# A two-layer decoder trunk on one core: the last two output tiles of each residual stage as token-half jobs, the norm behind them and the next quad by token halves

## What is computed

```python
hn = rmsnorm(x, norm1_g) * (1.0 + sc1) + sh1
proj = hn @ w_in                       # 1024 -> 2560, split in xl, gl, bs, cs, hs
...                                    # convolutions, gates, a recurrence -> lru_out, sc_out
mix = jnp.concatenate([lru_out, sc_out], axis=-1) @ w_out
x = x + g1 * mix
hn2 = rmsnorm(x, norm2_g) * (1.0 + sc2) + sh2
u, v = jnp.split(hn2 @ ffn_w_up, 2, axis=-1)       # 1024 -> 2 x 2816
uc, new_fc = causal_conv(u, st_fc, ffn_conv_w)
x = x + g2 * ((jax.nn.gelu(uc) * v) @ ffn_w_down)
```

## Time and profile before

| | |
|---|---|
| time, median of 3 runs (lowest, highest) | 1374.34 us (1372.85, 1374.78) |
| the profiled execution: its own time | 1370.7 us |
| its span, first to last instruction | 1369.0 us |
| mean granted TensorE clock | 0.981 of 2.4 GHz |
| TensorE matmuls, busy | 1324.8 us, 97% |
| weight loads, busy | 1262.4 us, 92% |
| VectorE, busy | 701.0 us, 51% |
| ScalarE, busy | 467.1 us, 34% |

### The profile page before, as it was taken

One profiled execution on the slowest core, in us unless ns is written; L12 is line 12 of the kernel. 1 busy time (PEld: TensorE's weight loads), 2 busy tenths in 40 slices (PEclk: granted clock), 3 DMA queues, 4 the chain that ended last, 5 costly groups with the idle time before them and its releaser, 6 DMA issues.

```text
span 1369.0 us, 23539 instructions
## 1 busy us (share of the span) xinstructions
PE 1324.8 (97%) x9727; PEld 1262.4 (92%) x9727; DVE 701.0 (51%) x1212; ACT 467.1 (34%) x589; POOL 47.3 (3%) x94
## 2 busy tenths in 40 slices
PE   5799999999999999999989999998999999999998
PEld 3698888889999999999989888998999999999997
DVE  2753663475534544345577158447553354534556
ACT  4523652353321322222353257326331232222332
POOL 3000000000000000000020000000000000000001
PEclk8899999989999999999999999999999999999999
DMA  9444555512122122222232645321222212222212
GB/s 334 165 158 171 203 206 185 185 62 93 61 93 92 62 92 92 69 86 77 76 123 86 211 166 204 124 93 62 73 81 93 93 61 92 81 73 93 75 49 94
DMA packets 108663, 157.02 MB, mean 115 GB/s; under 512 B 3543, under 2 KB 100792, under 8 KB 102453
## 3 DMA queue, kind: packets, MB, share of 16 engines
q1 hardware_dynamic: 101269, 112.56, 24.6%
q0 software_dynamic: 7168, 43.47, 9.2%
q10 hardware_dynamic: 160, 0.05, 0.0%
HBM read 153.08 MB, written 2.99 MB: 114 GB/s over the span
## 4 chain that ended last, share of the span: by engine, by line
PE 94%; DVE 3%; DMA 2%; ACT 1%; issue 0%; DVEq 0%; SPq 0%; POOLq 0%; ACTq 0%
PE ps L335 29%; PE ps L337 28%; PE ps L336 28%; PE ps L394 3%; PE ps L481 1%; DMA ada_w<-in_w_ada 1%; PE ps L428 1%; PE ps L417 1%; DMA work<-in_w_ada 0%; PE ps L358 0%; DVE work L804 0%; PE ps L360 0%; PE ps L359 0%; DVE w_raw L1156 0%; PE ps L409 0%
## 5 line engine op out<-in xcount | busy, mean ns | idle before, releaser
L335 PE MATMUL ps<-norm_hi,w_hi 128*128 128x288 f32 x2048 | 612.5, 299 | 13.7 <-DVE norm_lo L777 13.3
L336 PE MATMUL ps<-norm_lo,w_hi 128*128 128x288 f32 x2048 | 606.6, 296 | 0.0
L337 PE MATMUL ps<-norm_hi,w_lo 128*128 128x288 f32 x2048 | 604.4, 295 | 0.0
L335 PEld LDWEIGHTS ps<-norm_hi,w_hi 128*128 128x128 f32 x2048 | 386.4, 189 | 33.6 <-issue 19.1
L337 PEld LDWEIGHTS ps<-norm_hi,w_lo 128*128 128x128 f32 x2048 | 388.1, 189 | 0.0
L336 PEld LDWEIGHTS ps<-norm_lo,w_hi 128*128 128x128 f32 x2048 | 387.0, 189 | 0.0
L335 PE MATMUL ps<-mid_hi,w_hi 128*128 128x288 f32 x904 | 268.7, 297 | 0.0
L336 PE MATMUL ps<-mid_lo,w_hi 128*128 128x288 f32 x904 | 266.7, 295 | 0.0
L337 PE MATMUL ps<-mid_hi,w_lo 128*128 128x288 f32 x904 | 265.8, 294 | 0.0
L767 DVE TENSOR_TENSOR w_lo<-w_raw,w_hi 128x2048 fp32r<-128x2048 f32 x92 | 210.6, 2290 | 95.0 <-ACT w_hi L539 94.8
L539 ACT ACTIVATE w_hi<-w_raw 128x2048 fp32r<-128x2048 f32 x92 | 175.6, 1909 | 163.7 <-PE ps L337 162.9
(11 more groups left out here) (189 smaller groups left out, 846.7 us busy)
## 6 DMA issues: line engine op xcount, KB each, us to landing
w_raw<-in_ffn_w_up SPq DMA_DIRECT2D x44, 1024.0 KB, 5.1
ada_w<-in_w_ada POOLq DMA_DIRECT2D x40, 1024.0 KB, 5.2
w_raw<-in_w_in SPq DMA_DIRECT2D x20, 1024.0 KB, 5.3
w_raw<-in_ffn_w_down SPq DMA_DIRECT2D x16, 1024.0 KB, 5.2
w_raw<-in_w_out SPq DMA_DIRECT2D x8, 1024.0 KB, 5.2
w_raw<-in_ffn_w_down SPq DMA_DIRECT2D x8, 768.0 KB, 4.6
work<-in_w_ada SPq DMA_DIRECT2D x4, 1024.0 KB, 10.8
work<-in_x_prompt SPq DMA_DIRECT2D x4, 512.0 KB, 5.1
```

The costliest lines, as they stand in the source:

```text
L335: T.matmul(out, WH[:, r, k, c:c + P], xh[:, k, h, :], start=start, stop=False)
L336: T.matmul(out, WH[:, r, k, c:c + P], xl[:, k, h, :], start=False, stop=False)
L337: last = T.matmul(out, WL[:, r, k, c:c + P], xh[:, k, h, :], start=False, stop=stop)
```

## The change

The residual stages keep six output tiles (`FM`) as they are. The last two (`NQ`) run as four jobs of 24 matmuls: first half of tile 6, first half of tile 7, then the second halves. The statistics of the first half stand inside the third job, its spread inside the fourth; those of the second half stand in the next quad. The norm runs first over the first half, for two chunks at a time (`k_pair`), then over the second. `first_quad` does the first half for tiles 0 and 1, then for tiles 2 and 3, and then the same for the second half. The statistics and spreads have banks 4 and 5. The copy of the spread to SBUF is gone. FFN groups are 6, 8, 8 in place of 8, 8, 6, so that the last has eight chunks. At the end, three of the six tiles of `y` are transposed and scaled before the second half's statistics, and `y` is stored in that order.

```diff
-    GROUPS = [8, 8, KF - 16]
+    GROUPS = [KF - 16, 8, 8]
...
+            def half_chunk(i, s, k, h, xh, xl):
+
+                r, c, out = i // 2, (i % 2) * P, PS[:, 2 * s + h, 0:HALF]
+                T.matmul(out, WH[:, r, k, c:c + P], xh[:, k, h, :], start=(k == 0), stop=False)
+                T.matmul(out, WH[:, r, k, c:c + P], xl[:, k, h, :], start=False, stop=False)
+                return T.matmul(out, WL[:, r, k, c:c + P], xh[:, k, h, :], start=False, stop=(k == KX - 1))
+
+            def half_tiles_of_last_two(pair, m, after):
+
+                pe.wait_ge(lo_done, pair + 3)
                 for h in range(2):
...
+                    for i in range(NQ):
+                        pe.wait_ge(psum_free[i], pair + 1)
+                        for k in range(KX):
+                            last = half_chunk(2 + i, i, k, h, MH, ML)
+                            if k == KX - 1:
+                                last.then_inc(tile_done if h else half_done, 1)
+                            after(h, i, k)
+
+            def first_quad(pair, m, after, last_bank):
+
+                for h in range(2):
+                    for tiles in ((0, 1), (2, 3)):
+                        for k in range(KX):
+                            if tiles[0] == 0 and k % 2 == 0:
+                                pe.wait_ge(norm_ready, m * 8 - 8 + h * 4 + k // 2 + 1)
...
+                            for i in tiles:
...
+                                last = half_chunk(i, i, k, h, NH, NL)
+                                if k == KX - 1 and h == 1:
+                                    last.then_inc(tile_done, 1)
+                            after(h, tiles[0], k)
...
+                def norm_in_jobs(m, free):
+
+                    def after(h, i, k):
+                        if (h, i, k) == (1, 0, KX - 3):
+                            pe.wait_ge(*free)
+                            norm_stats(m, 0)
+                        if (h, i, k) == (1, 1, 2):
+                            norm_spread(m, 0)
+                    return after
+
+                def norm_in_quad(m):
+
+                    def after(h, i, k):
+                        if (h, i, k) == (0, 2, 2):
+                            norm_stats(m, 1)
+                        if (h, i, k) == (0, 2, KX - 2):
+                            norm_spread(m, 1)
+                    return after
...
+                for i in range(4):
+                    tile(l * PL + 2 + T_UP[0] // 2, i, NH, NL, range(KX), reads=0 if i < 2 else 1)
...
+            def after_last(h, i, k):
+                if (h, i, k) == (1, 0, KX - 3):
+                    pe.wait_ge(ns_read, L * 6)
+                    norm_stats(L * 2 + 1, 0)
+                if (h, i, k) == (1, 0, KX - 1):
+                    y_tile(0)
+                if (h, i, k) == (1, 1, KX // 2 - 1):
+                    pe.wait_ge(std_ready, 4 * L + 1)
+                    y_tile(1)
+                if (h, i, k) == (1, 1, KX - 1):
+                    pe.wait_ge(y_rows, 1)
+                    y_tile(2)
...
+            pe.wait_ge(y_rows, 3)
+            norm_stats(L * 2 + 1, 1)
...
+                dve.wait_ge(rs_done, max(m * 2 - 1 + h, 2))
                 scaled(0)
...
+                for p in range(5):
+                    if p < 4:
+                        f, t = sm(halves(HID[p % 2])), sm(halves(T1[p % 2]))
+                        step(V.tensor_tensor(f, t, seqs(GS, p, h), ALU.mult))
+                        V.tensor_tensor(f, f, seqs(MOD[:, sh:sh + KX], p, h), ALU.add).then_inc(norm_f, 1)
+                    if p:
+                        dve.wait_ge(norm_hi, n + p)
+                        low(k_pair(NL, p - 1, h), halves(HID[(p - 1) % 2]), k_pair(NH, p - 1, h), norm_ready)
+                    if p < 3:
+                        scaled(p + 1)
+                    fill(p)
...
+            def end_of_first_half(l, e, t, c):
+
+                for i in range(FM, KX):
+                    half_residual(l, e, t, c, i)
+                    sum_square(e, i - 1)
+                sum_square(e, 7)
+                rstd(e + 2, 0)
+                half_residual(l, e, t, c, 8)
+
+            def end_and_norm(l, e, t, c, split1, sh):
+
+                m = e + 2
+                end_of_first_half(l, e, t, c)
+
+                def fill(p):
+                    if p == 0:
+                        half_residual(l, e, t, c, 9)
+                    if p == 1:
+                        sum_square(e, 8)
+                        sum_square(e, 9)
+                    if p in (2, 3):
+                        split_half(m, *split1, p - 2)
+                normalise(m, sh, 0, fill)
+                rstd(m, 1)
+                normalise(m, sh, 1, lambda p: None)
```

More of the change, by code:

```diff
@@ L338, in chunk, with tile @@
                 return last
-            def tile(pair, i, xh, xl, order, ready=None):
+            def tile(pair, i, xh, xl, order, ready=None, reads=1):
                 if i % 2 == 0:
                     pe.wait_ge(lo_done, pair + (i // 2 + 3))
-                pe.wait_ge(psum_free[i % 2], pair + (i // 2 + 1))
+                pe.wait_ge(psum_free[i % 2], pair + (i // 2 + reads))
                 for j, k in enumerate(order):
@@ L349, in tile @@
                 last.then_inc(tile_done, 1)
-            def last_tile(pair, order):
-                pe.wait_ge(psum_free[1], pair + 2)
-                for h in range(2):
-                    out = PS[:, 2 + h, 0:HALF]
-                    for j, k in enumerate(order):
-                        hi, lo = WH[:, 1, k, P:2 * P], WL[:, 1, k, P:2 * P]
-                        T.matmul(out, hi, MH[:, k, h, :], start=(j == 0), stop=False)
-                        T.matmul(out, hi, ML[:, k, h, :], start=False, stop=False)
-                        last = T.matmul(out, lo, MH[:, k, h, :], start=False, stop=(j == len(order) - 1))
-                    last.then_inc(tile_done if h else half_done, 1)
@@ new lines, in _ @@
+                    if g == 2:
+                        for i in range(2):
+                            tile(l * PL + 2 + T_DN[g] // 2, i, MH, ML, range(K))
+                    made += K
+                between = norm_in_jobs(l * 2 + 3, (ns_read, l * 6 + 6))
+                if l < L - 1:
+                    half_tiles_of_last_two(l * PL + T_DN[2] // 2 + FM // 2, l * 2 + 3, between)
+                    first_quad((l + 1) * PL, l * 2 + 3, norm_in_quad(l * 2 + 3), None)
+            def after_last(h, i, k):
[10 more added lines that the diff above has]
+                    y_tile(2)
@@ new lines, in end_and_norm @@
+            def end_and_norm(l, e, split1, sh, between):
+                m = e + 2
+                square(e, 6)
+                square(e, 7)
+                std(m, 0)
+                square(e, 8)
+                norm_round(m, sh, 0, 0)
+                square(e, 9)
+                norm_round(m, sh, 0, 1)
+                split_halves(*split1, part=0)
+                norm_round(m, sh, 0, 2)
+                split_halves(*split1, part=1)
+                norm_round(m, sh, 0, 3)
+                between()
+                std(m, 1)
+                for p in range(4):
+                    norm_round(m, sh, 1, p)
@@ L596, in _ @@
                 A(halves(SQ0[k % 2]), X[:, k], ACT.Square).then_inc(sq_ready, 1)
-            std(1)
+            for h in range(2):
+                std(1, h)
             for l in range(L):
@@ L609, in _ @@
             ada_rows(1, first=True)
+            for part in range(2):
+                split_halves(0, 1, part)
+            for h in range(2):
+                for p in range(4):
+                    norm_round(1, MOD_SH1, h, p)
             for l in range(L):
-                split_halves(l, 1)
-                norm_round(l * 2 + 1, l * 16, MOD_SH1)
+                split(l, 2)
                 for c in range(KH):
@@ L728, in _ @@
                         act.preload_act_table(ACT.Sqrt)
-                        for m in range(KX):
-                            square(l * 18 + 9, m)
+                        for m in range(FM):
+                            square(l * 2 + 1, m)
                             if m in (1, 3):
@@ L1056, in _ @@
                 split(l, 11)
-                for m in range(KX - 1):
+                for m in range(FM):
                     residual(done(l, T_WOUT + m), m % 2, X[:, m], lambda a_, b_, m=m: MOD[:, MOD_G1 + m, a_:b_],
```

401 lines of the change are left out of this document (204 added, 197 removed).

## The result

| | before | after |
|---|---|---|
| time, median (lowest, highest) | 1373.89 us (1372.85, 1374.78), 4 runs | 1385.6 us (1382.56, 1388.17), 4 runs |
| the profiled execution: time, span | 1370.7, 1369.0 us | 1382.56, 1380.9 us |
| TensorE matmuls, busy | 1324.8 us, 97% | 1330.5 us, 96% |

The ratio is 1.0085 with a 95% interval of 1.0066 to 1.0104: slower by 11.7 us. The forecast was 6.65 us, to 1381.0 with a range of 1374 to 1387: the direction was right, the time lies in the range, and the size was not right.

A forecast was written before the change was run, and what follows sets the result against it. TensorE, busy for 97% of the span, bounds the kernel, so its idle time and inserted work count. Terms sum to +6.0 us, with the clock +6.65, giving 1377.3 profiled and 1381.0 us as median; range 1374 to 1387.

The forecast's parts named there:

- Waits at the boundaries: Boundaries 1, 2, 3 follow layer 0's output projection, its FFN, layer 1's output projection: TensorE waits 6.2, 8.1, 8.1 us.
- the 15 that the forecast set as its test: Over the whole kernel, TensorE's waits for low parts summing below 15 us would show the prediction wrong.
- Light work: Statistics and spreads inserted among TensorE's matmuls at each boundary: 0.8 and 1.1 us each, 3.8 a boundary.
- rival (a): Statistics, spreads and transposes slip among dense matmuls at no cost: 14.5 us fall away, 1366.5 us; chance 0.12.
- Rival (b): Low parts not late at boundaries 2 and 3, waits of 0.7 and 2.1 vanish: 1375.4 us; chance 0.13.
- the term of 0.65: Fall of TensorE's clock at the three boundaries: 1.3 us a fall, half of one fall taken, 0.65 us.
- rival (c): Clock falls at all three boundaries and VectorE is late once in each quad by 0.5: 1386.3 us; chance 0.20.
- costs nothing while that holds: FFN group order 6, 8, 8 issues the same matmuls, splits and loads; free while weight loads have no wait.
- The tail: End of the kernel from tile six: 27.6 us against 26.3 for the old order with eight chunks, +1.3.
- +6.0: Sum without the clock: 0.1 at the start, 0.1, 2.3, 2.2 at boundaries 1 to 3, 1.3 in the tail.
- at the start: Start of the kernel: only the third pair late by 0.35 us against a removed 0.27, +0.1.

The follow-up runs named there:

- repeated run: The changed kernel run once more, unaltered, against the kernel before: 1385.88 us, ratio 1.0077.

## Why the prediction was right in direction and short in size

**Waits at the boundaries: right.** Forecast 0.7 (with a restart 0.8), 2.1, 1.0, 1.3, 2.55 and 0.3 at boundaries 2 and 3; measured 1.03, 2.20, 1.04, 1.31 and 2.66 at boundary 2 of the repeated run, where the clock was full in the first half, and nothing for the last. The first low part behind the last job's residual is VectorE's row at 709.05. At boundary 1 the forecast 0.9 became 1.09. The sum of waits for low parts, 16.1 us and 3.2 under another name, is above the 15 that the forecast set as its test.

**Light work: oversized.** 0.8 and 1.1 were charged, 0.68 and 0.97 measured between dense matmuls, so 3.3 a boundary and not 3.8. The term is real, and rival (a), that it is free, is refuted: it needed about a third of the charge, and 87% was measured. Rival (b), low parts in time at boundaries 2 and 3, is refuted by the 2.04.

**The clock: the term of 0.65 was mis-sized most.** The forecast gave each boundary a little over one chance in three at 1.3. The profiled execution shows a fall in all three second halves at 1.0 each (14.43 for 13.42), and one in the tail, 2.2, which had no term at all: 5.2 together. Even by its own chances the forecast was too low: three times a third of 1.3 is 1.3, and it took half of that. This is the clock part of rival (c). The rule of the Trainium skill that I set beside the sum (TensorE: Matmul & The Clock Gate, Why this matters for your kernels) would have left the clock up through these waits, all shorter than the old ones; 18 of 21 second halves below full clock behind 2.66 us decide against it here, while the three at 1.00 show that it does not fail each time. The mistake was mine as well: I took the falls as a share of one event, and did not see that behind the wait stands a dense half, where a slow clock costs time.

**The group order and the loads: "costs nothing while that holds" was the step that failed.** The weight loads indeed had no wait. But I looked only at them, and not at the loads of modulation weights that GpSimd issues. Nor was it the group order (1.0005): the quad by halves gave ScalarE and VectorE its first finished tile later, the split of pair 3 ended 5.2 us later, and a 1 MB load started ahead of the other. The stretches of the two mixing stages are longer by 2.2 + 0.4 = 2.6 us. Rival (c) had VectorE late for the splits; it looked for the wait in the quad, where none came, and so came near the measured time (1386.3) by luck, with the clock's half of its mechanism right and the other not.

**The tail: +1.3 forecast, +0.7 at full clock, +2.9 with the fall.** After the last matmul the forecast's 11.7 was 11.8 in the repeat; the statistics and transposes ahead of it cost (1366.78 - 1351.74) less 95 matmuls of 0.133, so 2.4, and not 3.1.

**The sum, corrected.** The forecast's +6.0 was too high by 0.45 at boundary 1, 0.2 each at boundaries 2 and 3 (light work 0.5 less, waits 0.3 more), 0.3 at the start and 0.6 in the tail: +4.25 is left. To it come the clock, 3.0 + 2.2 = 5.2, and the loads, 2.6, less 0.2 in the FFNs' bodies: 11.85, measured 11.9. Of the 5.2 by which 11.85 exceeds 6.65, the clock makes 5.2 - 0.65 = 4.55 and the loads 2.6; what was priced too high, with the 0.2, takes back 1.95. That the forecast lies as near as it does owes something to this: errors of 7.15 one way and 1.95 the other.

What stays open is when the clock falls behind a wait of 2.7 us and when not. No run here sets that apart: it differs between two executions of the same kernel at the same boundary.

## What to carry to other kernels

When a big wait is cut in pieces, find for each remaining piece the instruction that waits in line ahead of the one wanted: here moving some instructions within their engines' programs turned +0.8% into -1.05%. Price a wait ahead of a dense stretch with the clock it may cost, and one inside a stretch that is fed late without. An edit that makes an engine start later in one place moves the start of every load that this engine releases; list the other queues' loads that begin within a few us and see which comes first.

## What the runs showed of the hardware that was not expected

- Two loads of 1 MB on different queues: the modulation load landed in 5.2 us where the weight load began 0.7 or 2.6 us behind it, and in 8.6 and 7.6 us where it had begun 1.4 and 0.9 us ahead. With the weight load 2.2 to 5 us ahead it took 5.0 to 6.4 in the changed kernel's profile.
- A wait of 2.66 us was followed by a mean granted clock of 0.88 or 0.89 in 15 of 21 cases (all three in the changed kernel's profile), of 0.81 in three and of 1.00 in three, with 14.3 to 14.4, 15.5 to 15.6 and 13.4 us for the same 96 matmuls. A fall in the half that waits for its chunks cost 0.04.
- Small matmuls in a dense stream cost a little less than their rows between the stages (0.76 and 1.02): six of one column add 0.68 us to the stream, a spread of six 0.97, with the slower start of the matmul behind them counted (boundary 1 of the changed kernel).
